# A two-block language model layer on one core: no spacer passes, decays spread over blocks, a weight split before the softmax, first convolution taps on ScalarE

## What is computed

```python
# first block: GLA
proj = rms_norm(x) @ w_in                     # q 1024, k 1024, v 2048, r 2048, g_low 16
log_a = log_sigmoid(g_low @ w_gate_up + b_gate) / 16
cum = cumsum(log_a over the 64 tokens of a chunk); total = its last
k_dec = k * exp(total - cum)                  # the decays
state = exp(total) * state + k_dec^T v;  o = q @ state     # per chunk
x += (norm(o) * silu(r)) @ w_out
x += relu(rms_norm(x) @ w_up)**2 @ w_down
# second block
q, k, v, xr, gate_br, b, c, xs, g = split(rms_norm(x) @ w_in_2)
y_a = softmax(q k^T / sqrt(128) + bias[head]) v            # 8 heads, causal
xc  = conv(xr, 4 taps) + conv_b                            # per channel
a   = exp(-8 * sigmoid(xc wa + ba) * softplus(-lam))
h   = scan(a, sqrt(1 - a*a) * sigmoid(xc wx + bx) * xc)
y_b = h * gelu(gate_br)
y_c = b * conv(c * xs, 3 taps)
x += (sum of sigmoid(g) * (y @ w)) @ w_out_2
x += relu(rms_norm(x) @ w_mlp_up)**2 @ w_mlp_down
out = rms_norm(x)
```

## Time and profile before

| | us |
|---|---|
| median of 3 runs (lowest to highest) | 2568.31 (2568.26 to 2570.51) |
| profiled execution | 2568.39 |
| its span | 2566.6 |
| PE busy | 2546.3 (99%) |
| DVE busy | 1815.6 (71%) |
| ACT busy | 1348.3 (53%) |
| mean granted clock of PE | 0.997 |

### The profile page before, as it was taken

The page is one execution under the profiler, slowest core; times in us unless marked ns, Lnnn a source line. Parts: engine busy times, 40 slices in busy tenths (PEclk is TensorE's granted clock), DMA queues, the critical chain, the costliest instruction groups (busy, mean ns, idle before and its releaser), DMA issues.

```text
span 2566.6 us, 43594 instructions
## 1 busy us (share of the span) xinstructions
PE 2546.3 (99%) x15628; PEld 2336.8 (91%) x15628; DVE 1815.6 (71%) x2067; ACT 1348.3 (53%) x1635; POOL 95.8 (4%) x96
## 2 busy tenths in 40 slices
PE   9999999999999999999999999999999999999998
PEld 8889999999999999999899999999999999999997
DVE  6767877667666677866897666766777676676675
ACT  6546555444444455544675555555554444454454
POOL 1000020000000002200000000000110000000001
PEclk9999999999999999999999999999999999999999
DMA  7794666666666666775556666666666666666664
GB/s 231 169 207 147 201 202 200 204 199 202 198 197 204 202 198 197 220 216 179 165 173 210 198 202 201 196 196 206 203 198 202 198 196 204 196 202 204 199 200 144
DMA packets 507427, 504.65 MB, mean 197 GB/s; under 512 B 17907, under 2 KB 505608, under 8 KB 507336
## 3 DMA queue, kind: packets, MB, share of 16 engines
q1 hardware_dynamic: 506060, 501.79, 62.6%
q10 hardware_dynamic: 1276, 1.63, 1.5%
HBM read 499.69 MB, written 3.67 MB: 196 GB/s over the span
## 4 chain that ended last, share of the span: by engine, by line
PE 94%; DMA 3%; DVE 2%; ACT 1%; issue 0%; SPq 0%; DVEq 0%; ACTq 0%
PE acc L545 60%; PE acc L547 30%; DMA raw<-in_gla_w_in 3%; PE acc L540 2%; DVE wsp L1157 1%; PE acc L542 1%; DVE lat L1490 0%; ACT wsp L835 0%; DMA xtok<-in_x 0%; PE misc L658 0%; PE misc L673 0%; PE misc L776 0%; PE misc L627 0%; PE misc L675 0%; DVE lat L1486 0%
## 5 line engine op out<-in xcount | busy, mean ns | idle before, releaser
L1157 DVE TENSOR_TENSOR wsp<-raw,wsp 128x1024 fp32r<-128x1024 f32 x944 | 1164.7, 1245 | 491.1 <-ACT wsp L835 456.9
L545 PE MATMUL acc<-xs,wsp 128*128 128x512 f32 x4224 | 1394.0, 383 | 3.5 <-DVE wsp L1157 3.0
L835 ACT ACTIVATE wsp<-raw 128x1024 fp32r<-128x1024 f32 x944 | 991.9, 1058 | 610.2 <-PE acc L547 506.2
L547 PE MATMUL acc<-xs,wsp 128*128 128x256 f32 x4224 | 1151.5, 273 | 0.0
L545 PEld LDWEIGHTS acc<-xs,wsp 128*128 128x128 f32 x4224 | 798.7, 189 | 116.7 <-DVE wsp L1157 5.0
L545 PE MATMUL acc<-hs,wsp 128*128 128x512 f32 x2560 | 841.0, 382 | 0.0
L547 PEld LDWEIGHTS acc<-xs,wsp 128*128 128x128 f32 x4224 | 811.2, 192 | 0.4
L547 PE MATMUL acc<-hs,wsp 128*128 128x256 f32 x2560 | 697.8, 273 | 0.0
L545 PEld LDWEIGHTS acc<-hs,wsp 128*128 128x128 f32 x2560 | 483.9, 189 | 67.2
L547 PEld LDWEIGHTS acc<-hs,wsp 128*128 128x128 f32 x2560 | 491.5, 192 | 0.0
L1167 DVE TENSOR_TENSOR z<-acc,corr 128x512 f32<-128x512 f32 x246 | 200.2, 814 | 184.6 <-ACT corr L846 184.5
(11 more groups left out here) (243 smaller groups left out, 1051.6 us busy)
## 6 DMA issues: line engine op xcount, KB each, us to landing
raw<-in_w_in SPq DMA_DIRECT2D x224, 512.0 KB, 4.4
raw<-in_mlp_w_up SPq DMA_DIRECT2D x128, 512.0 KB, 4.0
raw<-in_mlp_w_down SPq DMA_DIRECT2D x128, 512.0 KB, 4.3
raw<-in_w_mlp_up SPq DMA_DIRECT2D x128, 512.0 KB, 4.0
raw<-in_w_mlp_down SPq DMA_DIRECT2D x128, 512.0 KB, 4.3
raw<-in_gla_w_in SPq DMA_DIRECT2D x96, 512.0 KB, 4.8
raw<-in_gla_w_out SPq DMA_DIRECT2D x32, 512.0 KB, 4.5
raw<-in_w_out SPq DMA_DIRECT2D x32, 512.0 KB, 3.8
```

The costliest lines, as they stand in the source:

```text
L545: pe.matmul(both, w_part(0, slot)[:, t, cols], taking_turns(x[:, k0 + k]), start=start, stop=False, skip_group_check=True)
L547: ins = pe.matmul(acc[:, g, j, 1], w_part(1, slot)[:, t, cols], taking_turns(x[:, k0 + k, 0]), start=False, stop=stop, skip_group_check=True)
L835: act.activation(w_part(0, slot), raw[:, slot], ACT.Copy).then_inc(hi_done, 1)
L1157: dve.tensor_tensor(w_part(1, slot), raw[:, slot], w_part(0, slot).bitcast(F32), ALU.subtract).then_inc(lo_done, 1)
```

## The change

All spacers go, with the table that placed them. In gv the scan is cut in two halves (gv2, gv3), and the suffix sums, the exponentials, the product with the keys and the last part of a softplus move to gv4, gv5, gv6 and gv7. In xr, scc and scx the first unit of the block after next is split at the end of the evacuation, ahead of the hooks, on ACT and on DVE (`PULLED`, `AHEAD_OF`), so that the next `evac` and `take` start with the second unit; the normalise of a head leaves the hook and stands behind the first low part of the next `take`. Bias add and row maximum become one instruction for each half of a head, with the factor of the scores put into q. The first tap of both convolutions becomes two ACT passes a block, with a semaphore there and one back.

```diff
@@ -514,14 +514,7 @@
 
-        BROKEN = {"gk": (1, 2, 3), "gv": (0, 1), "gq": (0, 2, 3), "gr": (0, 1, 2, 3), "k": (1,), "v": (0,), "xr": range(4),
-                  "scc": range(4), "scx": range(4), "br": (0,)}
-
-        def spacer(to):
-
-            pe.matmul(to[:, 0:SPACE], xs[:, 0, 0, 0:P], xs[:, 0, 0, 0:SPACE], start=True, stop=True, skip_group_check=True)
-
-        def gemm(b, units, g, x, ready, k0=0, tokens_out=False, mid=None, before=None, mid_unit=2, spaced=False):
+        def gemm(b, units, g, x, ready, k0=0, tokens_out=False, mid=None, before=None, mid_unit=2):
...
@@ -546,12 +539,6 @@
-                        if spaced is True and u == t == j == 0:
-                            spacer(acc[:, g, 1, 0])
-                        if spaced == "late" and u == 0 and (t, j) == (UK - 1, 0):
-                            spacer(flat[1])
-                        if mid and u == mid_unit + 1 and (t, j) == (UK - 1, 0):
-                            spacer(flat[1])
                 ins.then_inc(unit_used, 1)
                 if mid and u == mid_unit:
                     mid()
...
@@ -814,6 +800,9 @@
 
+    PULLED = ("xr", "scc", "scx")
+    AHEAD_OF = [(name, i) for name in PULLED for i in range(4) if (name, i) != ("xr", 0)] + [("br", 0)]
+
...
@@ -834,10 +823,10 @@
-        def evac(b, rnd, first, n, g, early=None, late=None):
+        def evac(b, rnd, first, n, g, early=None, late=None, split=0):
 
             ahead = look_ahead(rnd, first, n)
-            for r, s in ahead[:-1]:
+            for r, s in ahead[split:-1]:
                 split_hi(r, s)
             if early:
                 early()
...
@@ -951,7 +940,7 @@
-            if (name, i) == ("gv", 3):
+            if (name, i) == ("gv", 5):
                 act.activation(lat[:], lat[:], ACT.Exp, scale=1.0 / TEMP).then_inc(suffix_exp, 1)
...
@@ -1098,7 +1087,19 @@
-                evac(b, rnd, 0, 4, g)
+                evac(b, rnd, 0, 4, g, split=(name, i) in AHEAD_OF)
+            if name in ("xr", "scx"):
+                act.wait_ge(padded, i + (1 if name == "xr" else 5))
+                for j in range(2):
+                    kt = 2 * i + j
+                    if name == "xr":
+                        ins = act.activation(xc[:, kt], xpad[:, j, 0:T], ACT.Identity, scale=prm("lru_conv_w_2", kt),
+                                             bias=prm("lru_conv_b_2", kt))
+                    else:
+                        ins = act.activation(cc[:, kt], xpad[:, j, 1:1 + T], ACT.Copy, scale=prm("sc_conv_w_2", kt))
+                ins.then_inc(first_tap, 1)
+            if name in PULLED:
+                split_hi(*look_ahead(rnd + 1, 0, 4)[0])
             if name == "br":
...
@@ -1157,10 +1158,12 @@
-        def take(b, rnd, first, n, g, then=None):
-
-            for r, s in look_ahead(rnd, first, n)[:-1]:
+        def take(b, rnd, first, n, g, then=None, between=None, split=0):
+
+            for k, (r, s) in enumerate(look_ahead(rnd, first, n)[split:-1]):
                 split_lo(r, s)
+                if between and k == 0:
+                    between()
             if then:
...
@@ -1256,7 +1259,7 @@
-            if (name, i) == ("gv", 6):
+            if (name, i) == ("gv", 7):
                 softplus_rest()
...
@@ -1283,11 +1286,12 @@
-            if (name, i) == ("gv", 2):
+            if name == "gv" and i in (2, 3):
                 dve.wait_ge(zero_done, 3)
-                fl = [t[:].rearrange("p k t -> p (k t)") for t in (mn, segm, lat)]
+                part = slice((i - 2) * LKT // 2, (i - 1) * LKT // 2)
+                fl = [t[:, part].rearrange("p k t -> p (k t)") for t in (mn, segm, lat)]
                 own.done(dve.tensor_tensor_scan(fl[0], fl[1], fl[2], 0.0, ALU.mult, ALU.add))
-            if (name, i) == ("gv", 3):
+            if (name, i) == ("gv", 4):
                 by = [t[:].rearrange("p k (c s) -> p (k c) s", s=CHUNK) for t in (lat, mn)]
...
@@ -1299,7 +1303,7 @@
-            if (name, i) == ("gv", 4):
+            if (name, i) == ("gv", 6):
...
@@ -1443,12 +1447,9 @@
-                dve.scalar_tensor_tensor(out=attn[:, 0:P], in0=flat[1][:, 0:P], scalar=AD ** -0.5, in1=skew[:, s, P:T],
-                                         op0=ALU.mult, op1=ALU.add)
-                own.done(dve.scalar_tensor_tensor(out=attn[:, P:BW], in0=flat[1][:, P:BW], scalar=AD ** -0.5,
-                                                  in1=skew[:, s], op0=ALU.mult, op1=ALU.add))
-                dve.tensor_reduce(amax[:, 0:1], attn[:, 0:P], AX_X, ALU.max)
-                own.done(dve.tensor_reduce(amax[:, 1:2], attn[:, P:BW], AX_X, ALU.max))
+                dve.tensor_tensor_reduce(attn[:, 0:P], flat[1][:, 0:P], skew[:, s, P:T], 1.0, NEG, ALU.add, ALU.max, amax[:, 0:1])
+                own.done(dve.tensor_tensor_reduce(attn[:, P:BW], flat[1][:, P:BW], skew[:, s], 1.0, NEG, ALU.add, ALU.max,
+                                                  amax[:, 1:2]))
                 dve.tensor_scalar(amax[:], amax[:], -1.0, None, ALU.mult).then_inc(attn_max, 1)
...
@@ -1461,11 +1462,6 @@
-            if s < AH:
-                dve.wait_ge(attn_exp, s + 1)
-                own.done(dve.reciprocal(ainv[:], asum[:]))
-                dve.tensor_scalar(attn[:, 0:P], attn[:, 0:P], ainv[:, 0:1], None, ALU.mult)
-                dve.tensor_scalar(attn[:, P:BW], attn[:, P:BW], ainv[:, 1:2], None, ALU.mult).then_inc(attn_ready, 1)
             if 6 <= s <= 12 and s % 2 == 0:
...
@@ -1481,11 +1477,7 @@
-                    w = prm(weight[0], weight[1])
-                    if bias is not None:
-                        ins = dve.tensor_scalar(dst, src, w, bias, ALU.mult, ALU.add)
-                    else:
-                        ins = dve.tensor_scalar(dst, src, w, None, ALU.mult)
+                    continue
                 else:
...
@@ -1493,7 +1485,16 @@
+        def normalise(s):
+
+            dve.wait_ge(attn_exp, s + 1)
+            own.done(dve.reciprocal(ainv[:], asum[:]))
+            dve.tensor_scalar(attn[:, 0:P], attn[:, 0:P], ainv[:, 0:1], None, ALU.mult)
+            dve.tensor_scalar(attn[:, P:BW], attn[:, P:BW], ainv[:, 1:2], None, ALU.mult).then_inc(attn_ready, 1)
+
         def second(name, i, b, rnd, g):
+            s = {"xr": 0, "scc": 4, "scx": 8}.get(name, 99) + i
+
             def first_std():
...
@@ -1501,14 +1502,15 @@
                 own.done(dve.reciprocal(rstd[:], rtmp[:]))
                 dve.tensor_tensor(rstd[:], rstd[:], rres[:], ALU.mult).then_inc(rstd_done, 1)
                 dve.wait_ge(rstd_done, 4)
             if name in ("q", "k"):
-                scaled(pair(q2 if name == "q" else k2, i)).then_inc(qkv_ready, 1)
+                scaled(pair(q2 if name == "q" else k2, i), AD ** -0.5 if name == "q" else 1.0).then_inc(qkv_ready, 1)
                 dve.wait_ge(qkv_ready, i + 1 + (4 if name == "k" else 0))
             if name == "v":
...
@@ -1521,7 +1523,9 @@
-                own.done(scaled(xpad[:, :, CONV - 1:]))
+                scaled(xpad[:, :, CONV - 1:]).then_inc(padded, 1)
+                dve.wait_ge(padded, i + 1)
+                dve.wait_ge(first_tap, i + 1)
                 for j in range(2):
...
@@ -1531,7 +1535,9 @@
-                own.done(dve.tensor_tensor(xpad[:, :, CONV - 1:], h[:], pair(cc, i), ALU.mult))
+                dve.tensor_tensor(xpad[:, :, CONV - 1:], h[:], pair(cc, i), ALU.mult).then_inc(padded, 1)
+                dve.wait_ge(padded, 5 + i)
+                dve.wait_ge(first_tap, 5 + i)
                 for j in range(2):
...
@@ -1548,6 +1554,8 @@
+            if name in PULLED:
+                split_lo(*look_ahead(rnd + 1, 0, 4)[0])
...
```

More of the change, by code:

```diff
@@ L28 @@
 SLOTS = 4
-SPACE = 200
 PAIRS = KT // 2
@@ L265, in build @@
     sq_paired = sem("sq_paired")
+    padded, first_tap = sem("padded"), sem("first_tap")
     rcol_done, y_scaled_act = sem("rcol_done"), sem("y_scaled_act")
@@ L690, in straight @@
             gemm(b, units_of(rnd, 0, 4), g, xs, split_upto(PAIR0["x1"]), tokens_out=(name == "gv"), mid=mid,
-                 before=before, mid_unit=3, spaced="late" if (name, i) == ("gr", 4) else i in BROKEN.get(name, ()))
+                 before=before, mid_unit=3)
             hooks(name, i)
@@ L709, in down @@
             def down(c, i, b, rnd, g, last=False):
-                gemm(b, units_of(rnd, 0, 4), g, hs, split_upto(h_base + 8 * c), spaced=last and final and not (isinstance(i, int) and i < 2))
+                gemm(b, units_of(rnd, 0, 4), g, hs, split_upto(h_base + 8 * c))
                 if last and final:
@@ L781, in straight2 @@
             mid = norm(2, two=True) if (name, i) == ("q", 0) else None
-            gemm(b, units_of(rnd, 0, 4), g, xs, split_upto(PAIR0["x2"]), tokens_out=(name == "v"), mid=mid,
-                 spaced=i in BROKEN.get(name, ()))
+            gemm(b, units_of(rnd, 0, 4), g, xs, split_upto(PAIR0["x2"]), tokens_out=(name == "v"), mid=mid)
             hooks2(name, i)
@@ L1502, in first_std @@
```

(3 more changed lines are left out.)

## The result

The changed kernel takes 2585.66 us (median of 6 runs, 2579.25 to 2586.71) against 2568.31 before (6 runs, 2568.11 to 2570.51): a ratio of 1.0061, 95% interval 1.0049 to 1.0073 (the two medians alone give 1.0068). The profiled execution took 2583.67 with a span of 2581.8. The forecast was 2581.8 in 2570 to 2588, slower.

What follows compares the result with a forecast made beforehand. The prediction took TensorE (PE) to bound the kernel, busy 2546.3 of 2566.6 us. It summed 2568.4 - 1.8 (spacers) - 0.6 (first layer) + 14.1 (part 3) + 1.7 (clock) = 2581.8 us, range 2570 to 2588.

Steps and rivals of the forecast that it cites:

- Part 3: Blocks xr to br, second layer: pulled split and moved normalise make PE wait at the transposes; 14.1 us more in all.
- the ring of both halves: Second layer: low part, exponential, high part, second low part and normalise in series; 14.1 at head 4, period 12.98 us.
- 13.85: Forecast length in us of DVE's loop in xr, reciprocal to reciprocal, where before it was 13.49.
- Taps: Convolutions' first taps: 0.90 us a block on DVE, against two ACT passes of 0.84 and a 0.96 wait; no gain.
- Fused passes: Softmax on DVE: passes and hand-overs of 1.29 us shrink to 1.0, ends 0.7 and 1.3.
- Spread decays: First layer's gate: spreading brings nothing; only five spacers ahead of the first bias copy count, 0.6 us less.
- the change touches none of it: First layer, 80 to 180 us: loads, splits, evacuations and bias copies pace each other, 12.15 us a step, unaltered.
- Rival (c): First layer: the cycle of loads and bias copies loosens when DVE and ACT are quicker; 5.5 us less, 2576.3; chance 0.08.
- Spacers: Throwaway PE passes: sixteen on the path outside xr to br and the first layer's wait stretch, 0.11 each, 1.8 us less.
- Rival (e): 33 blocks without spacers run at 0.341 us a pair; 14 us more, 2596; chance 0.04.
- Clock: PE drops to the 1.2 GHz level once, after head 6's stall of 4.0 us; 1.7 us more.
- rival (d): Up to six stalls of 1.1 to 2.4 us also bring low clocks, 1.7 each; 2583.5 to 2592; chance 0.08.

Runs made afterwards that it cites:

- e1: Changed kernel with both moves undone (no split ahead of the softmax, normalise back in the hook); 2563.21 us, 0.9982 of the kernel before.
- e3: Changed kernel with only the pulled split undone, the normalise still behind the first low part; 2572.03 us, 1.0007 of the kernel before.
- e8: e7 with the first taps of both convolutions back on DVE; 2555.55 us, 0.9952 of the kernel before.
- e7: e1 without the bias copies in gv1 to gq0 (the edit of e5); 2560.81 us, 0.9971 of the kernel before.
- e12: e11 with the first taps back on DVE; 2571.82 us, 1.0010 of the kernel before.
- e11: Changed kernel without the bias copies in gv1 to gq0 (the edit of e5); 2577.60 us, 1.0033 of the kernel before.
- e6: e5 with the decays also spread over gv2 to gv7; 2560.77 us, 0.9970 of the kernel before.
- e4: Kernel before with only the decays spread over gv2 to gv7; 2569.36 us, 1.0003 of the kernel before.
- e2: Changed kernel with only the normalise put back into the hook, the split still pulled; 2570.35 us, 1.0001 of the kernel before.
- e10: e5 without the 37 spacers, nothing else; 2556.83 us, 0.9955 of the kernel before.
- e5: Kernel before without eight bias copies in gv1 to gq0; rows written once to HBM, spread in go blocks; 2559.67 us, 0.9968.

## Why the prediction was right, point by point

- **Part 3, the split ahead of the softmax: right in mechanism, place and size.** Eight waits, 15.2 us (some 16 forecast), the longest at head 6 with 3.78 (4.0). DVE's idle time ahead of the low part before the reciprocal is 2.00 (about 2). e1 to e3 with the changed kernel, each half present or absent, show that it is the ring of both halves. The seven distances from xr1 to scx0 add up to 102.38 (102.13 forecast), none more than 0.32 off. Two errors cancel within it: in the xr loop the taps cost 0.67 instead of 0.06 (from the start of the scaling pass, L1191 now and L1188 before, to the low part behind the taps 5.29, and 4.62 before), and the fused passes save 0.62 instead of 0.29; the 0.16 that the sum takes off for passes that queue less tightly is 0.13. That 13.85 came so near to 14.16 is in part luck.
- **Taps: the term that was mis-sized.** "0.96 with the hand-over: no gain" took the cost to be DVE's own wait. Measured, the taps cost 5.3 us (e8 against e7) and 5.8 (e12 against e11): a longer pass with a bias, and above all the gates and splits that queue behind the waiting tap on ACT. That queue was not named in the prediction. Some of its effect stood in the sum all the same, as late low parts in br0 to br2 without their cause: from scx3 to br2 the forecast has at most 34.5, the changed kernel 36.1, and e12, which keeps the ring and has no taps on ACT, 32.6.
- **Fused passes:** 0.67 instead of 1.0, just below the lower end. From e6 to e8 the three blocks from xr2 to scc1 together gain 1.4 us beyond the spacer in each, which fits.
- **Spread decays:** the forecast that they bring next to nothing held (e4, e6). The 0.6 less did not come: the way to gq2 is 0.54 longer than before (162.21 against 161.67), although the spacers there are gone; that is inside the "at worst 1 more". The eighth copy was issued at 168.23 (168.5 follows from 169.03 less 0.55), but only because this execution started without the early low clock; from first to eighth copy it is 86.10, where before it was 85.04. The steps are 11.52 to 12.89. Of PE's 6.5 us of waits 2.6 stand at third units (gv4, gv7, gq0), the kind that the forecast named, and 3.9 at the first units of gv5, gv6, gq0 and gq1. And "the change touches none of it" is too strong: with other timing around it the ring can take a quicker course, in which e2's and e3's eight copies take 80.23 and 80.43. Rival (c) gave that 0.08; the changed kernel's lowest run, 2579.25, may be one, but it has no profile.
- **Spacers:** the 1.8 was right. From gq2 to xr1 the changed kernel takes 0.96 less, and from br2 to the end 0.76 less. Rival (e) did not come, as the pairs of e10 show; its 0.341 is no row's (the pair behind the spacer of xr0 takes 0.35).
- **Clock:** the trace before does not show the lower level once, as the prediction took it. It shows it in 10 to 15 us too, where PE had waited 1.02 and 1.52, so "shorter stalls were not" was a misreading. One low clock was forecast behind head 6. The profile has one behind head 7 instead, at the price forecast, and e11 one behind each. That 2585.66 lies 2 us above the profiled 2583.67 may be a second low clock of rival (d); it may as well be the early one, which the profiled execution lacks. Other runs speak for the early one: those of e5 lie at 2559.24 to 2559.67 and 2560.90 to 2561.28, with no wait above 0.6 in either stretch, and the profiled one, with the early low clock, is of the upper group; that of e10, without it, is the lowest of its four. The mean granted clock (0.996 in four of the other five runs, 0.997 in one, 0.998 in the profiled one) does not decide it, for each profile also has the lower level in its last 5 to 8 us, as PE's work ends. Without profiles of those runs this is argued, not shown.

The sum was 3.9 below the median. In the profiles the span grew by 15.2: -1.30 by the early low clock, 0.54 in the first layer (-0.6 forecast), -1.72 for spacers (-1.8) and 17.68 from xr1 to br2 (at most 15.7, with the clock). So what the prediction missed is 2.0 us behind xr1, most of it the late low parts of br0 to br2, and 1.1 in the first layer; the early low clock hides 1.3 of it in the profiled time. The runs give much the same: as far as the parts add, part 3 by e11 against e7 (16.8, low clocks included), the taps by e7 against e8 (5.3), the spacers by e10 against e5 (-2.8) and the fused passes (-1.4, the profiles of e6 and e8 in three xr blocks) make 17.9 against a measured 17.35.

## What to carry to other kernels

Pulling work of the engines that feed the bounding one ahead of a short serial chain pays only if the chain stays shorter than a block: write the whole ring down, engine by engine, with every pass that stands in its way, and compare it with the block. When a pass moves to another engine, count what queues behind its wait there: here that was the larger part of 5 us. And where an engine seems to wait for local work, look first at whether the loads that should have given it a lead came late.

## What the runs showed of the hardware that was not expected

- Eight copies of 192 KB out of one partition each kept 512 KB loads from HBM at 7.9 us to landing, instead of 4.3 without them (e5), and cost 7 to 9 us (7.1 between the profiled executions, 9.2 by the medians) although they move 1.5 MB in all. Read from one row in HBM, in other blocks, the same copies land after 4.1.
- The two fused passes (listed as CUSTOM_DVE_ANT_0) take 0.21 and 0.34 to the next start for 128 x 128 and 128 x 256, with accumulator reads of 0.08 beside them.
- An idle time of PE of 3.78 us was followed by the lower clock level in e11 (3.77 in e12) and not in the changed kernel's profile; one of 2.22 was followed by it in the changed kernel and e11 and not in e12. The length of a single wait did not decide it.
- Ahead of the first block, ten of fourteen profiles have the lower level for part of 5 to 15 us, and four have it nowhere there. The kernel before (0.66 in 10 to 15 us) and e4 (1.00) run the same program up to that point.
